# Where the element-wise products of an expert layer stand between the weight splits of ScalarE and VectorE

## The reference, cut to what matters

```
for e in range(N_EXPERTS):                       # 16 experts, D_FF_EXPERT = 512
    hidden = silu(xt @ w_exp_gate[e]) * (xt @ w_exp_up[e])
    y = y + combine[:, e:e + 1] * (hidden @ w_exp_down[e])
```

## Time and profile before

| what | us |
|---|---|
| median of 3 runs | 1787.03 (1785.43 to 1787.12) |
| the profiled execution | 1789.96 |
| its span, first to last instruction | 1788.2 |
| PE busy in the span | 1737.7 (97%) |
| DVE busy | 1311.7 (73%) |
| ACT busy | 949.8 (53%) |

### The profile page before, as it was taken

The page is one execution under the profiler, slowest core; times in us unless marked ns, Lnnn a source line. Parts: engine busy times, 40 slices in busy tenths (PEclk is TensorE's granted clock), DMA queues, the critical chain, the costliest instruction groups (busy, mean ns, idle before and its releaser), DMA issues.

```text
span 1788.2 us, 31815 instructions
## 1 busy us (share of the span) xinstructions
PE 1737.7 (97%) x12246; PEld 1517.7 (85%) x12246; DVE 1311.7 (73%) x1983; ACT 949.8 (53%) x1551; POOL 6.1 (0%) x6
## 2 busy tenths in 40 slices
PE   8999999999999999999999999999999999959997
PEld 5788888777878999999999999999999977636665
DVE  5989999996777886678666785577777776425776
ACT  4335765764356664456446564455555465325555
POOL 0000000000000001000000000000000000000000
PEclk9999999999999999999999999999999999979999
DMA  9957987986521467666666366665656469969983
GB/s 352 290 188 230 312 283 240 295 292 195 148 82 48 127 203 202 194 188 179 198 189 199 109 188 200 193 194 171 183 153 186 146 233 363 342 225 330 359 312 118
DMA packets 520688, 386.30 MB, mean 216 GB/s; under 512 B 15337, under 2 KB 477810, under 8 KB 520562
## 3 DMA queue, kind: packets, MB, share of 16 engines
q1 hardware_dynamic: 519904, 383.77, 67.7%
q10 hardware_dynamic: 658, 0.83, 0.1%
HBM read 380.35 MB, written 1.05 MB: 213 GB/s over the span
## 4 chain that ended last, share of the span: by engine, by line
PE 80%; DVE 9%; DMA 4%; ACT 3%; issue 3%; SPq 0%; ACTq 0%; DVEq 0%
PE ps L3210 16%; PE ps L3211 16%; PE ps L3212 16%; PE ps L4044 3%; DVE lo L1998 2%; DVE macc L2122 2%; PE ps L4018 2%; PE ps L3225 2%; PE ps L3224 2%; PE ps L3226 2%; PE ps L4019 2%; PE ps L4020 2%; PE ps L4074 2%; PE ps L4054 1%; PE ps L4055 1%
## 5 line engine op out<-in xcount | busy, mean ns | idle before, releaser
L1998 DVE TENSOR_TENSOR lo<-raw,hi 128x1024 fp32r<-128x1024 f32 (+2 forms) x384 | 459.4, 1198 | 87.2 <-ACT hi L1401 86.6
L1401 ACT ACTIVATE hi<-raw 128x1024 fp32r<-128x1024 f32 (+2 forms) x388 | 396.1, 1026 | 189.1 <-PE ps L3212 132.1
L3210 PE MATMUL ps<-nhi,hi 128*128 128x256 f32 (+1 forms) x1472 | 411.3, 279 | 0.0
L3211 PE MATMUL ps<-nlo,hi 128*128 128x256 f32 x1472 | 409.9, 278 | 0.0
L3212 PE MATMUL ps<-nhi,lo 128*128 128x256 f32 (+1 forms) x1472 | 409.2, 278 | 0.0
L3210 PEld LDWEIGHTS ps<-nhi,hi 128*128 128x128 f32 x1472 | 277.9, 189 | 2.4 <-issue 1.2
L3212 PEld LDWEIGHTS ps<-nhi,lo 128*128 128x128 f32 x1472 | 277.5, 189 | 0.0
L3211 PEld LDWEIGHTS ps<-nlo,hi 128*128 128x128 f32 x1472 | 277.3, 188 | 0.0
L3210 PE MATMUL ps<-hhi,hi 128*128 128x256 f32 (+1 forms) x576 | 174.9, 304 | 0.3 <-DVE lo L1998 0.3
L3211 PE MATMUL ps<-hlo,hi 128*128 128x256 f32 (+1 forms) x576 | 174.2, 302 | 0.0
L3212 PE MATMUL ps<-hhi,lo 128*128 128x256 f32 (+1 forms) x576 | 174.2, 302 | 0.0
(11 more groups left out here) (578 smaller groups left out, 3287.7 us busy)
## 6 DMA issues: line engine op xcount, KB each, us to landing
raw<-in_ffn_w_gu SPq DMA_DIRECT2D x176, 512.0 KB, 4.6
modw<-in_w_mod SPq DMA_DIRECT2D x56, 1024.0 KB, 6.6
raw<-in_ffn_w_d SPq DMA_DIRECT2D x64, 512.0 KB, 4.1
raw<-in_w_in SPq DMA_DIRECT2D x36, 512.0 KB, 4.4
mod_early<-in_w_mod SPq DMA_DIRECT2D x12, 1024.0 KB, 9.8
raw<-in_ffn_w_d SPq DMA_DIRECT2D x32, 384.0 KB, 3.6
raw<-in_attn_w_qkv SPq DMA_DIRECT2D x24, 512.0 KB, 4.0
raw_more<-in_w_exp_gate SPq DMA_DIRECT2D x20, 512.0 KB, 7.1
```

What stands on the lines that cost most here:

```text
L1401: nc.scalar.activation(hi[:, u * PITCH + at:u * PITCH + at + nk * P], raw[:, u * SLOT:u * SLOT + nk * P], ACT.Copy).then_inc(hi_ready, 1)
L1998: v.tensor_tensor(lo[:, s], raw[:, u * SLOT:u * SLOT + nk * P], hi[:, s].bitcast(F32), ALU.subtract).then_inc(lo_ready, 1)
L3210: pe.matmul(bank(u, T + more), w_hi(u, k, at), h_, start=(j == 0), stop=False)
L3211: pe.matmul(bank(u, n_lo), w_hi(u, k, at), l_, start=False, stop=False)
```

## The change

Three things change; the amount of work stays the same but for one ScalarE instruction.

- The distance of `due` becomes 4 splits, and 3 where the split that it counts from is of a step's one-block part. It stands on both engines for everything that `moe_step` places.
- In the one-block step PE takes wide slab 4, then the narrow slabs 6 and 7, then the wide slabs 5, 6 and 7; and the narrow products are turned after wide slab 6, not 7.
- A one-element SiLU on ACT ahead of split 8, which only brought the table in, is gone.

```diff
@@ up_groups
             if t == 1 and first == 0:
                 return ((0, 1), ()), ((2, 3), (0, 1, 2, 3))
+            if t == ONE_BLOCK and first:
+                return ((4, 5), (4,)), ((6, 7), (5, 6, 7))
@@ due
-            return next((q for q in range(RING, len(SPLIT)) if USED[SPLIT[q - RING]] >= used), len(SPLIT))
+            p = next((p for p in range(len(SPLIT)) if USED[SPLIT[p]] >= used), len(SPLIT))
+            single = p < len(SPLIT) and any(SPLIT[p][1] in (up_pair(ONE_BLOCK, c), down_pair(ONE_BLOCK, c % DOWN_SLABS)) for c in range(UP_SLABS))
+            return min(p + (3 if single else 4), len(SPLIT))
@@ narrow_turn
-            return HALF_UP + (3 if t == ONE_BLOCK else 2)
+            return HALF_UP + 2
@@ scalar moe_step
-                if q == 2 * U:
-                    nc.scalar.activation(rootc[:, :], epsc[:, :], ACT.Silu)
@@ vector moe_step
-                        if q == due(turned_at(t_, b)) - (0 if t_ else 3):
+                        if q == due(turned_at(t_, b)) - (0 if t_ else 1):
```

## The result

| what | before | after |
|---|---|---|
| median of the runs | 1786.97 (1785.43 to 1787.12, 4 runs) | 1758.03 (1757.79 to 1761.04, 4 runs) |
| span of the profiled execution | 1788.2 | 1759.2 |
| PE's idle time in the expert part, by its waits | 24.6 | 2.4 |

The ratio of the two is 0.9844, 95% interval 0.9827 to 0.9861: 28.9 us faster. The forecast was 27.0 us faster, at 1760.0.

A forecast was written before the change was run, and what follows sets the result against it. Bound: a loop in which ACT waits for transfers, PE for ACT and SP's queue for PE, plus the slowed clock. Terms summed to 27.5 us, taken as 27.0: 1787.0 - 27.0 = 1760.0 us; 8-in-10 range 1755 to 1771.

The forecast's parts named there:

- gaps and clock up to the narrow down product: One-block step: PE's three waits shrink and slow clock among them goes, so the narrow down product starts 22.1 us earlier.
- low clock behind it: Narrow down group after the one-block step's last gap: runs at full clock again, 2.4 us won if the clock stays up.
- step 3's narrow copies: Step 3: copies move from behind split 75 to behind 73, so the wait before the narrow down product goes, 2.5 us.
- the wait for hf: Step 4: DVE's gated product moves ahead of two splits, so PE's wait for it goes, 0.9 us.
- the sums' copies: Copies uhi and ulo for both wide blocks: the shorter distance makes split 103 late, 0.4 us lost, at most 1.5.
- The first two gaps: One-block step: PE's waits of 8.60 and 7.30 us for the narrow and wide SiLUs vanish once these stand behind earlier splits.
- The third gap: One-block step, before the narrow down product: 2.3 us remain of 4.54, as copies wait for a slab landing at 1578.4.
- kept: After the one-block step: slabs are in by 1596.2 and PE reads them from about 1600, so the later gains stand.
- Nothing: PE's new group order in the one-block step and removing the lone table-loading SiLU are worth nothing.
- A: Rival, chance 0.20: step 2's feed is thinner, the gap moves and costs clock, step 3's gap stays; 1766 to 1772 us.
- B: Rival, chance 0.04: slower, as products waiting for PE hold later splits; 1798 us with 2 us late at each SiLU.
- C: Rival, chance 0.04: no change, as PE waits for its own narrow slabs instead; about 1783 to 1787 us.

The follow-up runs named there:

- before_silu_both: Kernel before with only the three SiLUs of the one-block step moved three splits earlier on ACT: 1773.06 us, ratio 0.9916.
- others_lead_2: Kernel after with the places in steps 1, 3, 4 and 5 two splits earlier (distance two, not four): 1776.39 us, ratio 0.9931.
- sums_six: Kernel after with the copies of the finished sums back at splits 104 and 105, from 102 and 103: 1757.99 us, ratio 0.9824.
- order_back_places_kept: Kernel after with PE's old order and the table load back, narrow products pinned at split 48 and narrow copies at 50: 1758.88 us.
- others_lead_3: Kernel after with one split less of distance in steps 1, 3, 4 and 5 (three, not four): 1764.72 us, ratio 0.9871.
- others_old: Kernel after with every SiLU, product, copy and sum outside the one-block step back at distance six: 1764.08 us, ratio 0.9864.
- order_and_table_back: Kernel after with PE's old order and the table-loading SiLU back, places left to `due`: 1762.97 us, ratio 0.9862.
- one_block_old: Kernel after with the one-block step's SiLUs, gated products and copies back at their old places, PE's new order kept: 1779.03 us, ratio 0.9954.

## Why the prediction was right

The sum, term by term, by the table of the result:

| term | predicted | measured |
|---|---|---|
| gaps and clock up to the narrow down product | 22.1 | 23.4 |
| low clock behind it | 2.4 | 2.4 |
| step 3's narrow copies | 2.5 | 2.5 |
| the wait for hf | 0.9 | 1.1 |
| the sums' copies | -0.4 | -0.6 |
| sum | 27.5 | 28.9 |

The first measured term holds 0.2 us that were there ahead of the first gap. The forecast took 0.5 off its sum; the sum as added up was nearer.

**The first two gaps.** Right, by the mechanism named. The narrow SiLU was to start at 1564.05 and started at 1562.11, since split 44 came 1.95 us earlier than before (1561.14); the wide one was to be done by 1566.7 and was done at 1565.6. before_silu_both shows that it is the SiLUs' place alone that removes the two gaps.

**The third gap** is the term that was mis-sized: 2.3 us were to remain, 1.08 did. From the slab's landing to PE's start the forecast had 2.42 us; it took 2.44 (1577.04 to 1579.48; 2.42 from ACT's split, which is how the forecast counted). The landing itself was 1.4 us earlier than the 1578.4 worked out. That number started from a transfer's landing in the one profiled execution of before, and there the queue stood latest of all. The time from PE's narrow group (1558.43 before, 1558.21 after) to ACT's split 46, which starts when its slab has landed (1570.81 before, 1569.50 after), differs between executions, and the gap at mh_small follows it in every kernel in which the copies stand at split 50:

| kernel | split 46 after the narrow group | gap at mh_small |
|---|---|---|
| others_lead_2 | 11.01 | 0.81 |
| sums_six | 11.14 | 0.93 |
| after | 11.29 | 1.08 |
| order_back_places_kept | 11.50 | 1.34 |
| others_lead_3 | 11.92 | 1.66 |
| others_old | 12.05 | 1.81 |
| before | 12.38 | (2.3 forecast) |

The difference of the two columns is 10.16 to 10.26 in all six, so at 12.38 the gap would be 2.2. The step's working was right; its starting point was a sample of something that moves by 1.4 us. Each kernel has one profile, so how much of this moves with the kernel isn't known; before, others_old and before_silu_both have the same places up to the issue of this transfer and lie at 12.38, 12.05 and 11.19.

**The clock.** The 2.4 us came back. That the clock holds through a gap of 2.3 us wasn't put to the test by 1.08 us, and the runs speak less for it than the one row did: it held (1.00, or four matmuls in 1.08 us) behind 1.08, 1.34, 1.66, 1.81, 2.45 (before_silu_both, step 3) and, in before, 2.47 us; it fell behind 2.75, 3.70, 3.98 and 4.54, and it also fell behind single gaps of 1.77 us (order_and_table_back) and 2.02 us (others_lead_2), both shorter than the 2.47 that it survived. So between 1.77 and 2.47 us these runs show both outcomes. With the gap of 2.3 us that was forecast, the 2.4 us could have been lost; that they weren't is in part the luck of the earlier landing. The Trainium skill, "TensorE: Matmul & The Clock Gate", section "HAM oscillation — how this bites in real kernels", has the long waits throttle the engine; these rows agree for the long ones.

**The later gaps.** 2.5 and 0.9 were right as differences to the kernel before, but not as what this part of the change is worth. others_old shows 8.6 us. Against before, one_block_old and others_old remove 8.3 and 20.4 us; of the 8.3, up to 4.9 belongs to PE's order and 3.1 to the later gaps less the sums' cost, near the forecast. The step "kept" in the prediction (transfers keep up behind the step) was right for PE: neither after nor in others_old does it wait for a transfer there. What came late in others_old is the slab behind which the old places put the copies.

**What the shorter distance costs.** Right in place and nearly in size: 0.57 us at the sums, shown by sums_six. Elsewhere nothing at four; at three, 2.1 us from step 3's last narrow up group to smat. The 3.2 us chain against 4.2 us of lead was the right comparison: one split less, 2.8 us, and it no longer fits.

**"Nothing".** For the table load right. For PE's order wrong as a reason: I counted it at nothing because the copies wait for another thing, but without it DVE's product falls behind that same thing (2.9 us). That is the step of the prediction's reasoning that failed. It didn't hurt the sum, which was worked out with the places that the whole change gives.

**The rivals.** A (the gap moves, 1766 to 1772) didn't come. It did in before_silu_both: that is what the change would be without the moved products and copies. B (late splits) is real at a distance of three and two. The rule given with it, of the Trainium skill, "TensorE: Matmul & The Clock Gate", section "Architectural detail: the array is 16× 32×32, not 1× 128×128", that ACT and DVE work strictly in order, agrees with the 7.98 us for which one SiLU held step 0's copies. C (PE waits for its narrow slabs) is refuted: no DMA wait of PE stands in the expert part.

**The signs named.** sg_small 0.97 us after its split: yes, though 2.6 us ahead of PE's end of the gate and not at it. SP's stop of 3.5 us: 2.7. No PE gap over 1 us up to the narrow down product: yes. One of 1.5 to 4 us there: 1.08, smaller. PEclk 1.00: yes. PE's gaps 2 to 4 us: 2.4. A short gap at splits 103 to 105: 0.28. By the letter this is also one of the signs of being wrong, a lo split as PE's releaser in a step with two wide blocks; it is one wait, at the place that the sum had counted.

## What to carry to other kernels

In an engine that works in order, a piece's place is a choice of which transfer it waits for. List, for each piece that the bottleneck engine waits for, what stands ahead of it and when that data lands: here one split (four places against three, 3.2 us) decided, though ACT was idle nearly half the time. When a long stall goes, work out the waits behind it again: with the first two gaps gone and nothing else moved, the third grew from 4.5 to 7.8 us. And pull a piece forward only to the point where it is last behind data that is already there; beyond that it holds the splits for everyone else (+2.1 us at three, +8.8 at two in the last steps). Treat a landing read from one profile as good to about one slab, and don't count on the clock behind a gap because a gap of that length once left it alone.

## What was not expected of the hardware

- The same slab landed 11.0 to 12.4 us after the same PE instruction in thirteen profiled executions, in kernels with the same order of transfers up to there: a spread of 1.4 us, more than one slab's 1.27 us, and it passes one to one into the next gap that ends on a transfer.
- Single pieces of idle time of 1.77 us (order_and_table_back) and 2.02 us (others_lead_2) brought the clock down to 1.2 GHz for some 3 us, where single pieces of 2.45 us (before_silu_both) and 2.47 us didn't. So the length of a gap alone doesn't decide. What does wasn't tried by itself and stays open.
